# Second attention of a two-block model: head pairs in the value product, q packed as pairs, rope once for four heads

## Chip, cores and metric

One core of a Trainium2 chip runs the whole kernel. The metric is device time in microseconds (us); lower is better. The kernel before takes 1873.75 us (median of 3 runs).

## What is computed

The reference is two transformer-like blocks on 512 tokens of width 1024. The change lies in the causal attention of the second one: 16 heads, each with a query of 64 plain numbers and 32 that are turned by position (rope), a key of 64 plain numbers with 32 turned ones that all heads share, and a value of 64 numbers. Cut to this part:

```python
q = (rmsnorm_2(q_lat, q_norm_g[l]) @ w_uq[l]).reshape(B, S, 16, 64 + 32)
q_rope = rotary(q[..., 64:], positions)
q = jnp.concatenate([q[..., :64], q_rope], axis=-1)
kv = (rmsnorm_2(kv_lat, kv_norm_g[l]) @ w_ukv[l]).reshape(B, S, 16, 64 + 64)
k_nope, v = kv[..., :64], kv[..., 64:]
k_r = jnp.broadcast_to(rotary(k_rope, positions)[:, :, None, :], (B, S, 16, 32))
y_mla = causal_block_attention(q, jnp.concatenate([k_nope, k_r], -1), v)
merged = (jax.nn.sigmoid(g_rnn) * (y_rnn @ w_proj_rnn[l])
          + jax.nn.sigmoid(g_mla) * (y_mla @ w_proj_mla[l]))
```

## The kernel before

**Layout.** Activations lie transposed: 128 channels on the partitions, 512 tokens along the free axis, one such tile in one PSUM bank (`B[0]` to `B[7]`). `F(i)` and `R(i)` are the same SBUF tile `i` as fp32 and as fp32r.

**Blocks.** Every large product runs in blocks: one 128x128 weight block against 512 tokens, as three fp32r matmuls (high weights by high and by low activations, low weights by high activations: L251, L252, L253). The weights come as one stream in the order of use, 8 blocks a chunk, 286 chunks. For each chunk the SP queue loads `raw` (L2363), ScalarE (ACT) makes `whi` (L813), and VectorE (DVE, L1371) or, around the attention, GpSimd (POOL, L2150) makes `wlo`. `prep` and `start_of` set how far ahead each engine does this, and `until` does so for SP.

**Attention.** The order of work of each engine is written out by hand, head by head, `h` from 0 to 15. In head `h` TensorE (PE) turns the probabilities of head `h` (`mturn`, 4 groups of transposes, L653), multiplies them by the values (`mtimes`, key blocks 0 to 3, L667: two records for each fp32 matmul) and computes the scores of head `h+1` (`mscore`, L638, and the mask L640, token blocks `n` = 3, 2, 1, 0 with 512, 384, 256 and 128 keys). Between these stand 8 blocks of other products (`side`): the q projection of head `h+2` (`up_q`, 3 blocks), for every second head the k projection of two heads (`up_k`, 2 blocks), and the gate projection (`fill`), 64 blocks over the whole attention. DVE finds each score's maximum (`mmax`, L2014), ACT takes the exponential (`mexp`, L1236), DVE divides by the sum (`mnorm`, L2020 and L2021). Scores alternate between banks 3 and 4, so `mscore(h+1, 1)` waits until `mexp(h+1, 3)` has read bank 3.

**q and its rope.** `up_q(h)` makes one head: 96 rows used of 128, an odd head with rope rows 0 to 31 and plain rows 64 to 127. `q_copy` (ACT, L1214) brings all 128 rows to `QM[h % 2]`; then `mrope(h)` makes four DVE instructions on 32 rows (L2005, L2006, L2008, L2009) before bank 0 may be used again. `mnorm(h+1, 0)`, for which the next `mturn` waits, stands behind `mrope(h+2)` on DVE.

**Values.** `mtimes(h, kb)` writes partitions 0 to 63 of bank 7 for an even head and 64 to 127 for an odd one. After each odd head ACT and DVE take bank 7 away as the high and the low part of `YM` (`ym_hi` L1263, `ym_lo` through L1398). Transposed probabilities go through three buffers `PTM`, copied by ACT (L1249) and DVE (L2030).

**After it.** `first_pm` begins the output projection during head 15, and then `merged` is formed in `GMLA`: L2072 multiplies, L2075 adds the recurrent branch, which had been stored to `spare2` and is loaded into tiles `GR2` (L2454: six tiles after `until("uq", 8)`; L2459: two tiles after `until("pm", 2)`). The residual is loaded by L2463 right behind those.

Of the kernel before, what the change touches and what calls it, by code (L numbers as in the profile page):

```python
# [22 lines left out]
NCHUNK = 286  # L23
# [28 lines left out]
for _sem, _kinds in {  # L52
# [7 lines left out]
        "lru_dve": "lru_m lru_b lru_xv lru_h conv krsh kr_set",  # L60
# [87 lines left out]
QM, KM, PM, PTM, RM = (70, 71), (75, 78), 34, (39, 40, 41), (79, 74)  # L148
GR2 = [24, 25, 26, 27, 28, 29, 70, 71]
# [19 lines left out]
def program(nc, blocks, wst, xT, pT, small, consts, pos1, pos2, cT, wadaT, bcmp, ccmp, gblk, spare, spare2, us, ys, out):  # L169
    ctx = ExitStack()  # L170
    with ctx:
# [64 lines left out]
        def tensor(e):  # L236
# [358 lines left out]
            def up_q(h, ks):  # L595
                if ks[0] == 0:
                    if h == 0:
                        e.wait_ge(*at("pr_ev", 0))
                        for k in range(3):
                            e.wait_ge(*at("oplo", "ql", k))  # L600
                    else:
                        e.wait_ge(*at("mshq", h - 1))
                proj("uq", h, B[0], QL, ks)

            def up_k(h, ks):
                if ks[0] == 0:
                    if h == 0:
                        e.wait_ge(*at("pr_ev", 1))
                    else:
                        e.wait_ge(*at("km", h - 1))  # L610
                proj("uk", h // 2, B[1], KL, ks)

            def fill(n):
                for f in range(fills[0], fills[0] + n):
                    if f % 8 == 0 and f < 64:
                        if f:
                            e.wait_ge(*at("gmla", f // 8 - 1))
                        else:
                            e.wait_ge(*at("pr_ev", 2))
# [4 lines left out]
            def mscore(h, n):  # L624
                bk, w = B[3 + (n + 1) % 2], (n + 1) * 128
                K = slice(0, 96) if h % 2 == 0 else slice(0, 128)
                if n == 3:
                    e.wait_ge(*at("kr_set"))
                    e.wait_ge(*at("mrope", h))
                    e.wait_ge(*at("km", h))  # L630
# [24 lines left out]

            def mtimes(h, kb):
                rows_ = slice(64 * (h % 2), 64 * (h % 2) + 64)
                c0 = kb * 128
                e.wait_ge(*at("mptv" if kb == 1 else "mpt", 4 * h + kb))
                if kb == 0 and h % 2 == 0 and h:  # L660
                    e.wait_ge(*at("oplo", "ym", h // 2 - 1))
                if h == 0 and kb == 0:
# [3 lines left out]
                vo = h % 8 * 64  # L666
                e.matmul(B[7][rows_, c0:512], F(VS[h // 8][kb])[:, vo:vo + 64], F(PTM[(4 * h + kb) % 3])[:, c0:512],  # L667
                         start=kb == 0, stop=True, skip_group_check=True).then_inc(*sig("mpv", h, kb))

            def side(h, x):  # L670
                if h % 2 == 0:
                    if x < 2:
                        up_k(h, [x])
                    elif x < 5:
                        up_q(h, [x - 2])
                    else:
                        fill(1)
                elif x < 3:
                    up_q(h, [x])
                else:  # L680
                    fill(1)
# [3 lines left out]
            up_k(0, [0])  # L685
            up_k(0, [1])
# [9 lines left out]
            up_q(1, [0, 1, 2])  # L696
# [3 lines left out]
            def first_pm():  # L700
                f = pms[0]
                pms[0] += 1
                if f == 0:
                    e.wait_ge(*at("mshq", 15))
# [5 lines left out]
            for h in range(16):  # L710
                def work(x):
                    if h < 14:
                        side(h + 2, x)
                    elif h == 14:
                        fill(1)
                if h < 15:
                    work(0)
# [4 lines left out]
                    work(1)  # L722
                    mtimes(h, 0)
                    mscore(h + 1, 1)
                    work(2)
                    mscore(h + 1, 0)
                    work(3)
                    mturn(h, 2)
                    mtimes(h, 1)
                    work(4)  # L730
                    work(5)
                    mturn(h, 3)
                    work(6)
                    mtimes(h, 2)
                    mtimes(h, 3)
                    work(7)
# [68 lines left out]
        def scalar(e):  # L805
# [403 lines left out]

            def q_copy(h):  # L1210
                e.wait_ge(*made("uq", h))
                if h >= 2:
                    e.wait_ge(*at("msc", h - 2, 0))
                e.activation(F(QM[h % 2]), B[0], ACT.Copy).then_inc(*sig("mq", h))  # L1214

            def k_copy(h):
                e.wait_ge(*made("uk", h // 2))
                for x in (h, h + 1):
                    if x >= 2:
                        e.wait_ge(*at("msc", x - 2, 0))  # L1220
                    rows_ = slice(64 * (x % 2), 64 * (x % 2) + 64)
# [1377 lines left out]
```

## Time and profile before

| | us |
|---|---|
| median of 3 runs (1873.26 to 1876.18) | 1873.75 |
| profiled execution, own time | 1876.76 |
| its span, first to last instruction | 1875.0 |
| TensorE busy in the span | 1851.1 |
| VectorE busy | 1058.8 |
| ScalarE busy | 753.8 |
| GpSimd busy | 276.3 |

The granted TensorE clock is 0.997 of full speed over the span. Matmuls are pipelined: a record's duration covers its latency too, so the cost of a matmul is the distance from its start to the next start, and that distance is how the timeline of PE is read.

### The profile page before, as it was taken

How to read it: one execution, taken by the hardware profiler on the slowest of the kernel's cores; microseconds unless marked ns; L12 is line 12 of the kernel's file. 1: busy time of each engine (PE TensorE's matmuls, PEld its weight loads, DVE VectorE, ACT ScalarE, POOL GpSimd, SP SyncE). 2: the span in 40 equal slices, each digit the busy share in tenths (PEclk: the TensorE clock that was granted, in tenths of full speed). 3: DMA queues.
4: the chain of work that ended last, by engine and by line, in shares of the span. 5: the costliest groups of instructions: out<-in, count | busy, mean ns of one | idle time of the engine just before them, and what ended most of it. 6: DMA issues, size and time to landing. Idle time of an engine off the chain costs nothing.

```text
span 1875.0 us, 21232 instructions
## 1 busy us (share of the span) xinstructions
PE 1851.1 (99%) x8304; PEld 1454.5 (78%) x8304; DVE 1058.8 (56%) x1574; ACT 753.8 (40%) x1192; POOL 276.3 (15%) x357
## 2 busy tenths in 40 slices
PE   9999999999999999999999999999999999999998
PEld 7888888778878888888877767666668788888886
DVE  8764553846575545553577592555535565435643
ACT  6554444443352212222434653444433344324431
POOL 4767535200000000000001021321210000000000
PEclk9999999999999999999999999999999999999999
DMA  5323222224235535542423223212114223233321
GB/s 208 102 74 96 68 85 88 83 86 156 91 128 203 193 133 205 194 152 78 140 73 109 78 79 118 96 34 79 46 44 148 79 92 100 79 106 97 90 83 63
DMA packets 64403, 199.44 MB, mean 106 GB/s; under 512 B 7152, under 2 KB 11504, under 8 KB 64304
## 3 DMA queue, kind: packets, MB, share of 16 engines
q1 hardware_dynamic: 64304, 198.09, 32.1%
q8 instruction: 66, 1.08, 0.2%
q14 instruction: 33, 0.27, 0.0%
HBM read 189.68 MB, written 8.39 MB: 106 GB/s over the span
## 4 chain that ended last, share of the span: by engine, by line
PE 71%; issue 21%; DVE 6%; ACT 2%; DMA 0%; POOL 0%; SPq 0%; POOLq 0%; DVEq 0%; ACTq 0%
PE bank L251 20%; PE bank L253 20%; PE bank L252 20%; PE bank L638 2%; PE bank L667 2%; PE bank L653 1%; DVE wlo L1371 1%; PE bank L544 1%; PE bank L297 1%; PE bank L340 1%; PE bank L356 1%; DVE tiler L1398 1%; DVE tile L1906 1%; ACT whi L813 0%; PE bank L377 0%
## 5 line engine op out<-in xcount | busy, mean ns | idle before, releaser
L251 PE MATMUL bank<-tiler,whi 128*128 128x512 f32 x2272 | 917.8, 404 | 6.7 <-DVE wlo L1371 1.5
L253 PE MATMUL bank<-tiler,wlo 128*128 128x512 f32 x2272 | 897.1, 395 | 0.0
L252 PE MATMUL bank<-tiler,whi 128*128 128x512 f32 x2272 | 896.6, 395 | 0.0
L813 ACT ACTIVATE whi<-raw 128x1024 fp32r<-128x1024 f32 x285 | 300.1, 1055 | 605.6 <-PE bank L253 599.3
L251 PEld LDWEIGHTS bank<-tiler,whi 128*128 128x128 f32 x2272 | 427.2, 188 | 126.7 <-issue 21.2
L253 PEld LDWEIGHTS bank<-tiler,wlo 128*128 128x128 f32 x2272 | 427.0, 188 | 102.1
L252 PEld LDWEIGHTS bank<-tiler,whi 128*128 128x128 f32 x2272 | 427.7, 188 | 97.0 <-issue 3.1
L1371 DVE TENSOR_TENSOR wlo<-raw,whi 128x1024 fp32r<-128x1024 f32 x262 | 325.4, 1246 | 281.9 <-ACT whi L813 281.5
L2159 POOL TENSOR_TENSOR stat<-stat,scl 128x4 f32<-128x4 f32 x7 | 7.8, 1111 | 1127.6 <-DVE stat L1389 698.4
L2150 POOL TENSOR_TENSOR wlo<-raw,whi 128x1024 fp32r<-128x1024 f32 x23 | 54.5, 2371 | 249.2 <-ACT whi L813 249.2
L2098 DVE SCALAR_TENSOR_TENSOR tile<-bank,sm,tile 128x511 f32<-128x511 f32 x44 | 33.0, 749 | 98.0 <-ACT tile L1345 62.5
L1398 DVE TENSOR_TENSOR tiler<-tile,tiler 128x512 fp32r<-128x512 f32 x109 | 73.9, 686 | 4.5 <-ACT tiler L1100 2.1
L823 ACT ACTIVATE tile<-tile 128x512 f32<-128x512 f32 x45 | 28.3, 629 | 102.2 <-DVE tile L2130 39.9
L1789 DVE CUSTOM_DVE_ANT_0 wide<-wide 128x1024 f32<-128x1024 f32 x48 | 58.5, 1220 | 0.0
L1236 ACT ACTIVATE wide<-bank,stat 128x512 f32<-128x512 f32 (+1 forms) x64 | 33.5, 525 | 46.7 <-DVE stat L2014 46.7
L2014 DVE TENSOR_REDUCE stat<-bank 128x1 f32<-128x512 f32 (+1 forms) x64 | 30.8, 489 | 31.8 <-PE bank L640 30.0
L638 PE MATMUL bank<-tile 96*128 96x384 f32 (+7 forms) x128 | 45.7, 452 | 0.0
L2130 DVE SCALAR_TENSOR_TENSOR tile<-bank,mod,tile 128x512 f32<-128x512 f32 x16 | 11.9, 751 | 58.8 <-PE bank L253 58.8
L667 PE MATMUL bank<-tile 128*64 128x512 f32 (+3 forms) x128 | 44.9, 452 | 0.0
L1818 DVE TENSOR_TENSOR tile<-tile,bank 128x512 f32<-128x512 f32 x22 | 15.1, 686 | 43.7 <-PE bank L253 41.0
L1345 ACT ACTIVATE tile<-bank,sm 128x512 f32<-128x512 f32 x22 | 17.1, 779 | 53.8 <-PE bank L253 53.8
L1832 DVE TENSOR_TENSOR tile<-tile,bank 128x512 f32<-128x512 f32 x16 | 11.0, 687 | 47.6 <-PE bank L253 47.6
(364 smaller groups left out, 1635.5 us busy)
## 6 DMA issues: line engine op xcount, KB each, us to landing
raw<-wst SPq DMA_DIRECT2D x285, 512.0 KB, 3.6
wide<-wadaT SPq DMA_DIRECT2D x48, 512.0 KB, 3.5
tile<-xT SPq DMA_DIRECT2D x16, 256.0 KB, 6.1
spare<-tile SPq DMA_DIRECT2D x16, 256.0 KB, 2.0
tile<-spare SPq DMA_DIRECT2D x16, 256.0 KB, 5.0
out<-tile SPq DMA_DIRECT2D x8, 256.0 KB, 2.0
tile<-gblk SPq DMA_DIRECT2D x5, 256.0 KB, 4.6
us<-tile SPq DMA_DIRECT2D x4, 256.0 KB, 2.0
```

What stands on the lines that cost most here:

```text
L251: e.matmul(bank, whi[:, o:o + 128], hi, start=start, stop=False)
L252: e.matmul(bank, whi[:, o:o + 128], lo, start=False, stop=False)
L253: e.matmul(bank, wlo[:, o:o + 128], hi, start=False, stop=stop).then_inc(*sig("blk", n))
L638: e.matmul(bk[:, 0:w], F(QM[h % 2])[K, n * 128:(n + 1) * 128], F(KM[h % 2])[K, 0:w], start=True, stop=True, skip_group_check=True)
L667: e.matmul(B[7][rows_, c0:512], F(VS[h // 8][kb])[:, vo:vo + 64], F(PTM[(4 * h + kb) % 3])[:, c0:512], start=kb == 0, stop=True, skip_grou ...
L813: e.activation(whi[:, c % NHL * W:(c % NHL + 1) * W], raw[:, c % NRAW * W:(c % NRAW + 1) * W], ACT.Copy).then_inc(*sig("hi", c))
L1236: e.activation(prob(h, n), B[3 + (n + 1) % 2][:, 0:w], ACT.Exp, bias=stat[:, ST_MM + z + n:ST_MM + z + n + 1], accum_out=stat[:, ST_MD + z ...
L1371: e.tensor_tensor(wlo[:, h:h + W], raw[:, c % NRAW * W:(c % NRAW + 1) * W], whi[:, h:h + W].bitcast(F32), SUB).then_inc(*sig("lov", c))
L1398: e.tensor_tensor(R(lo), src, R(hi).bitcast(F32), SUB).then_inc(*sig("oplo", name, k))
L1789: e.tensor_tensor_reduce(w, w, F(CR, 2), 1.0, 0.0, MUL, ADD, F(PART)[:, m:m + 1]).then_inc(*sig("ada", m))
L2098: then(e.scalar_tensor_tensor(out=F(t)[:, 1:512], in0=bk[:, 0:511], scalar=col("fcw", 44 + mt), in1=F(t)[:, 1:512], op0=MUL, op1=ADD))
L2150: e.tensor_tensor(wlo[:, h:h + W], raw[:, c % NRAW * W:(c % NRAW + 1) * W], whi[:, h:h + W].bitcast(F32), SUB).then_inc(*sig("log", c))
```

## The change

Four edits that belong together:

1. The q weights are cut differently. `up_q(p)` makes the plain rows of a pair of heads (8 pairs, 24 blocks), and `up_r(g)` makes the rope rows of four heads (4 groups, 12 blocks). Before there were 16 heads with 48 blocks. The weight stream has 285 chunks.
2. `rope4(g)` multiplies, shuffles and multiplies all 128 rope rows of four heads with three DVE instructions; `mrope(h)` is then one addition of 32 rows into `QM`. `q_copy` copies 64 rows. `mnorm(h+1, 0)` now stands right behind `mnorm(h+1, 1)`.
3. `mtimes` runs in odd heads only and takes both heads of the pair, one behind the other, for each key block. `PTM` has eight buffers, four for each head of a pair.
4. The blocks of `side` are dealt out anew: 8 in the heads 0 to 2, 4 to 6, 8 to 10, 12 and 14 (in head 14: 8 of `fill`), 5 in the heads 3, 7, 11 and 13. `GR2` gets other tiles, and all its eight loads stand after `until("pm", 2)`.

Head 15 and all that follows keep their order. The diff, cut; on TensorE:

```diff
-QM, KM, PM, PTM, RM = (70, 71), (75, 78), 34, (39, 40, 41), (79, 74)
-GR2 = [24, 25, 26, 27, 28, 29, 70, 71]
+QM, KM, PM, PTM, RM = (70, 71), (75, 78), 34, ((24, 25, 26, 27), (28, 29, 39, 40)), (79, 74)
+GR2 = [66, 65, 64, 63, 62, 70, 71, 75]
...
+            def up_q(p, ks):
                 if ks[0] == 0:
-                    if h == 0:
+                    if p == 0:
                         e.wait_ge(*at("pr_ev", 0))
+                    elif p % 2:
+                        e.wait_ge(*at("mq", 2 * p - 1))
+                    else:
+                        e.wait_ge(*at("mshq", p // 2))
+                proj("uq", p, B[0], QL, ks)
+
+            def up_r(g, ks):
+                if ks[0] == 0:
+                    if g == 0:
+                        e.wait_ge(*at("pr_ev", 2))
                         for k in range(3):
                             e.wait_ge(*at("oplo", "ql", k))
                     else:
-                        e.wait_ge(*at("mshq", h - 1))
-                proj("uq", h, B[0], QL, ks)
-
-            def up_k(h, ks):
+                        e.wait_ge(*at("mq", 4 * g - 1))
+                proj("ur", g, B[0 if g else 2], QL, ks)
+
+            def up_k(p, ks):
                 if ks[0] == 0:
-                    if h == 0:
+                    if p == 0:
                         e.wait_ge(*at("pr_ev", 1))
                     else:
-                        e.wait_ge(*at("km", h - 1))
-                proj("uk", h // 2, B[1], KL, ks)
+                        e.wait_ge(*at("km", 2 * p - 1))
+                proj("uk", p, B[1], KL, ks)
...
-                e.matmul(B[7][rows_, c0:512], F(VS[h // 8][kb])[:, vo:vo + 64], F(PTM[(4 * h + kb) % 3])[:, c0:512],
-                         start=kb == 0, stop=True, skip_group_check=True).then_inc(*sig("mpv", h, kb))
+                for x in (h - 1, h):
+                    rows_ = slice(64 * (x % 2), 64 * (x % 2) + 64)
+                    vo = x % 8 * 64
+                    e.matmul(B[7][rows_, c0:512], F(VS[x // 8][kb])[:, vo:vo + 64], F(PTM[x % 2][kb])[:, c0:512],
+                             start=kb == 0, stop=True, skip_group_check=True).then_inc(*sig("mpv", x, kb))
...
             def side(h, x):
-                if h % 2 == 0:
-                    if x < 2:
-                        up_k(h, [x])
+                if h == 14:
+                    if x:
+                        fill(2 if x == 7 else 1)
+                elif h % 2 == 0:
+                    if x < 3:
+                        up_q(h // 2 + 1, [x])
                     elif x < 5:
-                        up_q(h, [x - 2])
+                        up_k(h // 2 + 1, [x - 3])
                     else:
                         fill(1)
-                elif x < 3:
-                    up_q(h, [x])
-                else:
+                elif h in (1, 5, 9):
+                    if x < 3:
+                        up_r((h + 3) // 4, [x])
+                    else:
+                        fill(1)
+                elif x not in (3, 5, 7):
                     fill(1)
```

In the head loop of PE the four calls of `mtimes(h, kb)` now stand under `if h % 2`. On ACT:

```diff
                     mexp(h + 1, 1)
-                    if h % 2 == 1 and h < 14:
+                    if h % 2 == 0 and h < 14:
                         q_copy(h + 2)
                     mexp(h + 1, 0)
                     if h % 2 == 0 and h < 14:
-                        k_copy(h + 2)
+                        q_copy(h + 3)
                 pt_copy(h, 2)
                 if h % 2 == 0 and h < 14:
-                    q_copy(h + 2)
+                    k_copy(h + 2)
+                    k_copy(h + 3)
```

On DVE:

```diff
+            def rope4(g):
+                bank = B[0 if g else 2]
+                e.wait_ge(*made("ur", g))
+                if g:
+                    e.wait_ge(*at("mrope", 4 * g - 1))
+                e.tensor_tensor(F(RM[0]), bank, F(RC2), MUL)
+                e.stream_shuffle(F(RM[1]), bank, SHUF).then_inc(*sig("mshq", g))
+                e.wait_ge(*at("mshq", g))
+                e.tensor_tensor(F(RM[1]), F(RM[1]), F(RS2), MUL).then_inc(*sig("mrot", g))
+
             def mrope(h):
-                rr = slice(64, 96) if h % 2 == 0 else slice(0, 32)
-                w1, w2 = F(RM[0])[rr, :], F(RM[1])[rr, :]
-                e.wait_ge(*at("mq", h))
-                if h:
-                    e.wait_ge(*at("mrope", h - 1))
-                e.tensor_tensor(w1, B[0][rr, :], F(RC2)[rr, :], MUL)
-                e.stream_shuffle(w2, B[0][rr, :], SHUF).then_inc(*sig("mshq", h))
-                e.wait_ge(*at("mshq", h))
-                then(e.tensor_tensor(w2, w2, F(RS2)[rr, :], MUL))
-                e.tensor_tensor(F(QM[h % 2])[rr, :], w1, w2, ADD).then_inc(*sig("mrope", h))
+                to = slice(64, 96) if h % 2 == 0 else slice(0, 32)
+                of = slice(32 * (h % 4), 32 * (h % 4) + 32)
+                e.wait_ge(*at("mrot", h // 4))
+                if h >= 2:
+                    e.wait_ge(*at("msc", h - 2, 0))
+                e.tensor_tensor(F(QM[h % 2])[to, :], F(RM[0])[of, :], F(RM[1])[of, :], ADD).then_inc(*sig("mrope", h))
...
+            e.wait_ge(*at("kr_set"))
+            rope4(0)
             mrope(0)
             pr_out(5)
             mmax(0, 3)
...
             mmax(0, 0)
             mnorm(0, 1)
             mrope(1)
+            mnorm(0, 0)
             pr_out(7)
             for h in range(16):
-                mnorm(h, 0)
...
                     mmax(h + 1, 0)
+                    if h < 14:
+                        mrope(h + 2)
                     mnorm(h + 1, 1)
-                if h < 14:
-                    mrope(h + 2)
+                    mnorm(h + 1, 0)
+                if h in (1, 5, 9):
+                    rope4((h + 3) // 4)
```

On SP:

```diff
-            until("uq", 8)
-            for m in range(6):
+            until("pm", 2)
+            e.wait_ge(*made("in2", 31))
+            for m in range(5):
                 e.wait_ge(*at("sp%d" % m, 0))
                 e.dma_start(F(GR2[m]), spare2[m]).then_inc(*sig("sp%d" % m, 1, by=16))
-            until("pm", 2)
             e.wait_ge(*at("msc", 15, 0))
-            for m in range(6, 8):
+            for m in range(5, 8):
```

## Rows read from the trace of the kernel before

**Rows 1.** Busy time by stretch, the attention: PE, PEld, DVE, ACT, POOL, clock, DMA.
```profile
1180.00:1412.00 232.00, 229.91 (x991) 145.41 (x990) 123.17 (x301) 106.34 (x249) 44.56 (x19) 1.00 0.20 64
```

**Rows 2.** Timeline of PE, end of heads 0 and 1: start, duration, instruction.
```profile
1211.00 0.40 PE L252 MATMUL bank<-tiler,whi 128*128 128x512 f32 x1
1211.23 0.40 PE L253 MATMUL bank<-tiler,wlo 128*128 128x512 f32 x1
1211.75 0.66 PE L653 MATMUL bank<-ident,wide 128*128 128x128 f32 x4
...
1223.97 0.40 PE L253 MATMUL bank<-tiler,wlo 128*128 128x512 f32 x1
1224.21 0.60 PE L653 MATMUL bank<-ident,wide 128*128 128x128 f32 x4
```

**Rows 3.** Timeline of PE, value products of head 0.
```profile
1201.96 0.40 PE L253 MATMUL bank<-tiler,wlo 128*128 128x512 f32 x1
1202.29 1.07 PE L667 MATMUL bank<-tile 128*64 128x512 f32 x2
1203.29 0.70 PE L638 MATMUL bank<-tile 128*128 128x256 f32 x2
...
1208.83 0.40 PE L253 MATMUL bank<-tiler,wlo 128*128 128x512 f32 x1
1209.16 0.86 PE L667 MATMUL bank<-tile 128*64 128x256 f32 x4
1209.95 0.50 PE L251 MATMUL bank<-tiler,whi 128*128 128x512 f32 x1
1210.29 0.39 PE L252 MATMUL bank<-tiler,whi 128*128 128x512 f32 x1
```

**Rows 4.** All weight loads of L667: duration ns min/median/max.
```profile
L667 PEld LDWEIGHTS bank<-tile x128: 132/136/137, 1202.3 to 1400.3; 128*64 128x64 f32 x128
```

**Rows 5.** Waits in the attention (1165 to 1412): us in total, times, longest.
```profile
PEld bank L653 <- DVE wide L2021: 4.9, 8, 1.0
```

**Rows 6.** Timeline of PE, first transposes of head 0.
```profile
1198.99 0.66 PE L653 MATMUL bank<-ident,wide 128*128 128x128 f32 x4 [0.54 <-DVE wide L2021]
```

**Rows 7.** Timeline of PE, DVE and ACT, first scores of heads 4 and 5.
```profile
1237.39 1.02 PE L638 MATMUL bank<-tile 96*128 96x512 f32 x2
1238.26 0.22 PE L640 MATMUL bank<-maskb,identb 128*128 128x128 bf16 x1
...
1239.24 0.69 ACT L1236 ACTIVATE wide<-bank,stat 128x512 f32<-128x512 f32 x1 [1.05 <-DVE stat L2014]
...
1240.20 1.07 PE L667 MATMUL bank<-tile 128*64 128x512 f32 x2
...
1249.81 1.02 PE L638 MATMUL bank<-tile 128*128 128x512 f32 x2
...
1250.93 0.69 DVE L1398 TENSOR_TENSOR tiler<-bank,tiler 128x512 fp32r<-128x512 f32 x1 [4.09 <-ACT tiler L1263]
...
1252.26 0.69 ACT L1236 ACTIVATE wide<-bank,stat 128x512 f32<-128x512 f32 x1 [0.87 <-DVE stat L2014]
```

**Rows 8.** Last instruction of `mrope`: duration ns min/median/max over 16.
```profile
L2009 DVE TENSOR_TENSOR tile<-tile x16: 678/682/2805, 1177.0 to 1371.5; 32x512 f32<-32x512 f32 x16
```

**Rows 9.** Timeline of DVE, q rope and last step of head 5's softmax.
```profile
1258.70 0.69 DVE L2005 TENSOR_TENSOR tile<-bank,tile 32x512 f32<-32x512 f32 x1 [2.53 <-ACT tile L1214]
...
1261.72 0.29 DVE L2021 TENSOR_SCALAR wide<-wide,stat 128x128 f32<-128x128 f32 x1
```

**Rows 10.** Timeline of SP, DVE and ACT after head 15; L2459's landing times.
```profile
1404.01 0.85 SPq L2459 DMA_DIRECT2D tile<-spare  x2
...
1407.65 0.69 DVE L2075 TENSOR_TENSOR tile<-tile 128x512 f32<-128x512 f32 x1
...
1426.20 1.06 ACT L813 ACTIVATE whi<-raw 128x1024 fp32r<-128x1024 f32 x1 [3.47 <-PE bank L253]
...
DMA to landing us min/median/max: 3.7/4.3/4.8
```

More of the change, by code:

```diff
@@ L22 @@
 NTILE = 80
-NCHUNK = 286
+NCHUNK = 285
 HALF_PI = math.pi / 2
@@ L710, in tensor @@
             for h in range(16):
-                def work(x):
-                    if h < 14:
-                        side(h + 2, x)
-                    elif h == 14:
-                        fill(1)
                 if h < 15:
-                    work(0)
+                    side(h, 0)
                     mturn(h, 0)
@@ L721, in tensor @@
                     mturn(h, 1)
-                    work(1)
-                    mtimes(h, 0)
+                    side(h, 1)
+                    if h % 2:
+                        mtimes(h, 0)
                     mscore(h + 1, 1)
-                    work(2)
+                    side(h, 2)
                     mscore(h + 1, 0)
-                    work(3)
+                    side(h, 3)
                     mturn(h, 2)
-                    mtimes(h, 1)
-                    work(4)
-                    work(5)
+                    if h % 2:
+                        mtimes(h, 1)
+                    side(h, 4)
+                    side(h, 5)
                     mturn(h, 3)
[L733 to L736, printed above, removed]
+                    side(h, 6)
+                    if h % 2:
+                        mtimes(h, 2)
+                        mtimes(h, 3)
+                    side(h, 7)
                 else:
@@ L1207, in scalar, with pair @@
                 e.activation(F(GRNN[m]), F(GRNN[m]), ACT.Sigmoid).then_inc(*sig("grnn_s", m))
+            def pair(x, to, bank, kind, scale):
+                if x >= 2:
+                    e.wait_ge(*at("msc", x - 2, 0))
+                rows_ = slice(64 * (x % 2), 64 * (x % 2) + 64)
+                e.activation(F(to[x % 2])[rows_, :], bank[rows_, :], ACT.Copy, scale=scale).then_inc(*sig(kind, x))
             def q_copy(h):
[L1211 to L1214, printed above, removed]
+                e.wait_ge(*made("uq", h // 2))
+                pair(h, QM, B[0], "mq", 1.0)
             def k_copy(h):
                 e.wait_ge(*made("uk", h // 2))
[L1218 to L1221, printed above, removed]
-                    e.activation(F(KM[x % 2])[rows_, :], B[1][rows_, :], ACT.Copy, scale=SC2).then_inc(*sig("km", x))
+                pair(h, KM, B[1], "km", SC2)
             def mexp(h, n):
@@ L1265, in scalar @@
             start_of("pr", 4)
-            start_of("uk", 0)
-            k_copy(0)
-            q_copy(0)
+            start_of("ur", 0)
+            for h in range(2):
+                k_copy(h)
+            for h in range(2):
+                q_copy(h)
             start_of("pr", 5)
@@ L1273, in scalar @@
             mexp(0, 1)
[L1274 removed]
+            start_of("pr", 7)
             mexp(0, 0)
[L1276 to L1277 removed]
             for h in range(16):
[L1279 to L1282 removed]
+                if h % 2 == 0 and h < 14:
+                    start_of("uq", h // 2 + 1)
+                elif h in (1, 5, 9):
+                    start_of("ur", (h + 3) // 4)
+                elif h < 15:
+                    start_of("in2", 24 + h // 2)
                 if h % 2 == 0 and h:
@@ L1289, in scalar @@
                     mexp(h + 1, 1)
-                    if h % 2 == 1 and h < 14:
+                    if h % 2 == 0 and h < 14:
                         q_copy(h + 2)
```

54 lines of the change are left out of this document (18 added, 36 removed).

## The prediction

> **What bounds the kernel.** I read part 1 of the page first: TensorE is busy for 1851.1 of 1875.0 us, and no other engine for more than 1058.8. The windows say the same of the stretch that is changed: from 1180 to 1412 us PE is busy for 229.91 of 232 us, DVE for 123.17, ACT for 106.34, at full clock [rows 1]. So the time is the sum of PE's own distances from start to start, plus the few places where PE waits. The timeline of PE gives the distances. Inside a block one matmul follows another after 0.23 us, and a transpose group that waits for nothing follows a block after 0.24 [rows 2]. A block of three is thus 0.70 us. Work taken from DVE or ACT buys nothing by itself; it counts only where one of them released PE late. The waits show one such place, the division by the sum (L2021) before the first transposes of a head, 8 times [rows 5].
>
> **Part 1, the blocks.** 48 q blocks become 24 + 12 = 36. Twelve blocks at 0.70 us are 8.4 us. All stood in PE's gapless stream, so nothing hides them: -8.4 us. They fall out of heads 3, 7, 11 and 13, three each, at places where the softmax of the next head has been issued; these heads get two heads' value products in exchange, so they do not become short. The ScalarE and DVE share of the one or two chunks fewer is off the path: 0.
>
> **Part 2, the value products.** Now every head pays for three visits to L667. The first: block to L667 0.33 us instead of 0.23, then 1.00 us to the next start [rows 3]. The third, 256 + 128 columns: again 0.33, then 0.79, and the block behind it has 0.34 instead of 0.23 between its first two starts [rows 3]. What the columns themselves take I scale from the 512-column score, 0.87 us from L638 to its mask [rows 7]: 0.87 for the first visit, 0.65 for 384 columns. So a visit costs beyond its columns 0.10 + 0.13 = 0.23 us for the first, and 0.10 + 0.14 + 0.11 = 0.35 for the third. The second also has 384 columns; behind transposes I take 0.27 (without the 0.08 that leaving any fp32 work costs). That is 0.85 us a head. Two heads in one visit pay it once: 8 x 0.85 = -6.8 us. Bounds: 0, if changing from one half of the array's columns to the other costs as much as entering, and -6.8.
>
> Then the columns. Each matmul is two passes with a weight load of 0.136 us each [rows 4]. Head A's second pass must follow its first, since both use the same columns of the array. Head B writes the other 64 partitions, so B's first pass could run beside A's second: three pass times instead of four. The trace of before never has two such neighbours, so it shows neither this nor its absence. Bounds from rows: nothing, or one pass of every key block, half of 0.87 + 0.65 + 0.65 = 1.08 us a pair, 8.7 us in all. Between them lies the case that B's weights are loaded only when A's second pass has started: each key block then saves its pass less 0.14, which is 0.29, 0.18 and 0.07 us for 512, 384 and 256 columns and nothing for 128, 0.54 us a pair, -4.3 us. I take this one, because a value product's records lie as load, matmul, load, matmul, and 0.136 us is longer than a 128-column pass.
>
> The Trainium skill bears on both halves. TensorEngine Tiling (Array Packing), section Key Properties, says that a change of tiling mode drains the array, while tiles of one mode work independently; by that page the first half is right and the second is the gain of up to 8.7 us. TensorE: Matmul & The Clock Gate, Part 3 (What overlaps and what doesn't), says against it that a weight load overlaps running matmuls only where the row groups differ, and here both heads use all 128 rows; by that rule alone the columns give nothing. The excess of 0.10 to 0.14 us around L667 agrees with the drain [rows 3].
>
> **Part 3, rope and the old waits.** `mrope` was four DVE instructions of about 0.68 us [rows 8] behind a copy, and the last division waited for it: PE's last start of head 0 is 1211.23, the transposes start 0.52 us later instead of 0.24, and take 0.05 longer to start up [rows 2]. About 0.33 us, in the 7 such heads that the waits count besides the first [rows 5]: 2.3 us. Before head 0 the idle time is 0.54 us at the least [rows 6], with the same start-up and pipeline loss about 0.8; there `mnorm(0, 0)` now goes before `pr_out(7)`. Together -3.1 us (bounds -2.4 and -3.5). `rope4` is three instructions of 128 rows at some 0.7 us (the rows are parallel, the length is the same 512), in heads 1, 5 and 9 only, with several us until the next `up_q` of an even pair needs its bank. Two such instructions were held for 2.8 us once each [rows 8]; the slack below covers one.
>
> **Part 4, a new wait.** In an even head nothing stands any more between `side(h, 1)` and `mscore(h+1, 1)`, which needs `mexp(h+1, 3)`. In head 3 the value product that stood there started 2.81 us after the head's first score [rows 7], so the score would now be due after 2.7. ACT begins the exponential 1.85 us after the score, takes 0.69 and about 0.1 for the sum: 2.64, and with a weight load of 0.2 behind it PE loses about 0.2 us. In head 4 it begins only after 2.45 us, because DVE first makes the low part of `YM` (1250.93) [rows 7]: 3.24, a loss of 0.75. This delay stays where the head before has 8 blocks and its gate copy stands at the end (heads 2, 6, 10); after the 5-block heads it is hidden. 3 x 0.75 + 5 x 0.2 = +3.3 us (bounds 0 and 8 x 0.75 = 6).
>
> Behind that score nothing else of PE is late: an even head lasts 12.4 us now (1237.39 to 1249.81 [rows 7]), less 3.0 for its value products 9.4, plus the wait. Head 5's softmax ends 12.2 us after its first score, but DVE was free at 1258.70 - 2.53 = 1256.17, 6.4 us after it [rows 7, 9]. With one rope addition, the last division and the late start that is about 8 us, and the next transposes come after 9.0 to 9.7.
>
> **Part 5, loads of `GR2`.** Eight loads now start at about 1404.0 instead of two. The first lands 4.3 to 4.8 us later, 1408.3 to 1408.8, where L2075 wanted it at 1407.65 [rows 10]. DVE is up to 1.2 us late with an addition; PE needs only L2072, already done, of the banks: 0. Six more issues at 0.43 us delay the residual and the next weights by 2.6 us and by what their bytes take; ScalarE wants the weights in question at 1426.20, 22 us after the first issue, some 3 us earlier now that chunks end half a chunk later. If the six landed one after the other at 4.8 us each, 29 us, the loss would be up to 10 us; but two landed in the time of one. I take 0.
>
> **Sum.** -8.4 - 6.8 - 4.3 - 3.1 + 3.3 = -19.3 us, from the profiled execution's 1876.76 to 1857.5. That execution lies 3.0 us above the median of 1873.75, so the forecast is 1854.4 us. A measurement of this kernel can tell about 0.2% (3.7 us) from no change.
>
> **Rivals.**
> (a) The pair shares its visit, but not its time: no overlap of the columns, 1858.7. For it: both heads fill all rows, and PE starts its matmuls in order. Chance 0.25.
> (b) A full pass saved in each key block: 1850.0. For it: a load lies ahead of its matmul elsewhere too. 0.17.
> (c) The change of column half costs what the entry cost; neither saving exists: -8.4 - 3.1 + 3.3 = -8.2, 1865.5. The rows show the excess at each side of L667 and never within one half. 0.12.
> (d) Slower. The softmax chain, not PE, sets the length of even heads, because `q_copy(h+2)` waits for `up_q`'s third block and holds back `mexp(h+1, 0)`. If the chain kept its 12.2 us against the 9.1 at which it is due, 8 even heads would lose 3.1 us each, 25 us, and the kernel would end at about 1879. It decides from (19.3 + 3.7)/8 = 2.9 us of lateness per even head; against it, the chain held two copies and four rope instructions and now holds one copy and one addition. 0.03, and 0.03 more for a part of it that lands within 0.2%.
> (e) The weights after the `GR2` loads come late by up to 10 us: about 1864. 0.05.
> My forecast has 0.35.
>
> **Range.** 1849 to 1863 us holds the forecast, (a), (b) and the bounds of parts 3 and 4 about them; outside lie (c), (d) and half of (e). Faster by over 0.2%: 0.94, within: 0.03, slower: 0.03.
>
> **What would show it.** In the profile after: 36 fewer records each of L251 to L253 together (12 each), 49 visits to L667 turned into 25, and in an even head `mscore(h+1, 1)` as the only place with a wait, 0.2 or 0.75 us. Part 2 is read from the start distances of a pair's first visit: with 512 columns twice, about 1.87 us for (a), 1.6 for the forecast, 1.45 for (b), over 1.95 for (c). The 0.52 us before the transposes must be 0.24, and the next weights must arrive without idle time of PE between 1400 and 1430. The prediction is wrong if an even head lasts over 11 us, or if that first visit lasts 2 us.

## The result and the profile after

| | before | after |
|---|---|---|
| median, us | 1874.78 (4 runs, 1873.26 to 1876.18) | 1841.28 (4 runs, 1836.53 to 1841.46) |
| profiled execution, own time, us | 1876.76 | 1841.46 |

The ratio is 0.9817, 95% interval 0.9803 to 0.9831: 33.5 us less, where 19.3 were forecast, and 7.7 us below the lower end of the range. The direction was right; the size was not. In one series below the kernel before once took 2012.11 us, at a lower clock, and the pair-only kernel once 9313.93 us; the medians given are those of the other executions.

The stretch with the attention, in the windows of the kernel after (columns as in [rows 1]; it now holds some of what follows the attention too):

```profile
1180.00:1412.00 232.00, 230.57 (x1106) 161.44 (x1105) 118.80 (x279) 117.45 (x264) 40.72 (x18) 1.00 0.25 83
```

PE is as full as before and the clock is the same. It gets through 1106 matmul records in the 232 us where it had 991: the stretch is shorter because PE's own work is. So the difference has to be looked for in start distances. First visit of a pair's value products in head 1, and third visit, timeline of PE after:

```profile
1211.92 0.40 PE L253 MATMUL bank<-tiler,wlo 128*128 128x512 f32 x1
1212.25 1.08 PE L681 MATMUL bank<-tile 128*64 128x512 f32 x4
1213.26 0.70 PE L650 MATMUL bank<-tile 96*128 96x256 f32 x2
...
1218.82 0.40 PE L253 MATMUL bank<-tiler,wlo 128*128 128x512 f32 x1
1219.14 0.87 PE L681 MATMUL bank<-tile 128*64 128x256 f32 x8
1219.94 0.50 PE L251 MATMUL bank<-tiler,whi 128*128 128x512 f32 x1
1220.28 0.39 PE L252 MATMUL bank<-tiler,whi 128*128 128x512 f32 x1
```

L681 is the old L667. The first visit has four records and lasts 1.01 us from start to start; one head's two records lasted 1.00 [rows 3]. The third has eight and lasts 0.80; one head's four lasted 0.79. The forecast had 1.6 us for the first visit, and its most hopeful rival 1.45. The second head costs 0.01 us. Why is seen when the window is cut so narrow that only records which start between 1212.24 and 1212.30 are listed (PE), and in PEld's answer for the same visit:

```profile
1212.25 0.65 PE L681 MATMUL bank<-tile 128*64 128x512 f32 x2
```
```profile
1212.25 0.20 PEld L681 LDWEIGHTS bank<-tile 128*64 128x64 f32 x4 [0.36 <-issue]
```

Two of the four matmuls start within 0.06 us of each other: both heads' first passes. (They cannot be the two passes of one head: in the kernel before, the second record of a 512-column product starts 0.48 us after the first.) All four weight loads are over by 1212.45, 0.20 us after the visit's start, while the first passes, 0.65 us together, still run.

The old wait before the transposes [rows 2, 6] is gone in both places, with 0.23 and 0.24 us from the last block's start:

```profile
1199.51 0.40 PE L253 MATMUL bank<-tiler,wlo 128*128 128x512 f32 x1
1199.75 0.60 PE L665 MATMUL bank<-ident,wide 128*128 128x128 f32 x4
...
1208.79 0.39 PE L253 MATMUL bank<-tiler,wlo 128*128 128x512 f32 x1
1209.02 0.49 PE L665 MATMUL bank<-ident,wide 128*128 128x128 f32 x3
```

The new wait stands where part 4 put it, at `mscore(h+1, 1)`; timeline of PE in heads 0 and 2, then its row in the waits from 1165 to 1412:

```profile
1202.65 0.40 PE L253 MATMUL bank<-tiler,wlo 128*128 128x512 f32 x1
1202.89 0.67 PE L650 MATMUL bank<-tile 128*128 128x256 f32 x2
...
1224.34 0.40 PE L253 MATMUL bank<-tiler,wlo 128*128 128x512 f32 x1
1225.16 0.70 PE L650 MATMUL bank<-tile 128*128 128x256 f32 x2 [0.42 <-ACT wide L1254]
```
```profile
PE bank L650 <- ACT wide L1254: 1.4, 4, 0.4
```

Head 0 waits for nothing (0.24 us). Head 2 has 0.82, a loss of 0.58, and with the slower start behind it the head lasts 9.90 us from first score to first score instead of 9.28 in head 0, 0.62; heads 6 and 10 are like it, and head 14 loses 0.33: 2.2 in all.

What the kernel lost, added up from PE's starts between the first transposes of head 0 and the last value product: 201.45 us before, 166.87 after, -34.6.

| part | forecast | read from the trace after |
|---|---|---|
| 12 blocks | -8.4 | -8.4 |
| value products, visits and columns | -11.1 | -24.8 (8 x (1.10 + 1.00 + 1.00)) |
| late transposes, 7 heads | -2.3 | -2.3 |
| a wait of L251 for a gate copy in head 14 | not named | -0.85 |
| new wait | +3.3 | +2.2 |
| sum | -18.5 | -34.15 |

The three numbers in the second row are what a visit costs over a stream without it: the first 0.10 + 1.00, the third 0.10 + 0.79 + 0.11, both by [rows 3]; the second, behind transposes, 0.31 to its start and 0.79 to the block, less the 0.13 that the two transposes alone take (1205.22 to 1205.35), and 0.03 behind it. An even head without a wait agrees: 12.42 us from first score to first score in [rows 7] (1237.39 to 1249.81), 9.28 after in head 0 (1200.18 to 1209.46). What is left of the -34.6, 0.4 us, is not assigned. Outside this stretch the stall before head 0 [rows 6] gave back 0.7; of the 35.4 us between the two profiled spans the rest is +1.5 ahead of the attention, where a stretch at half clock is longer (see below), and -1.6 behind it, which is not assigned.

### The profile page after: what moved, and what is told of

The parts are those of the page before. It is cut to its first block, busy times and chain, and to the rows that moved or that the text cites. A ratio compares the mean times of both kernels' runs of the same rounds, so it can differ in the third digit from the quotient of the medians.

```text
span 1839.6 us, 21094 instructions
## 1 busy us (share of the span) xinstructions
PE 1815.2 (99%) x8268; PEld 1443.0 (78%) x8268; DVE 1032.6 (56%) x1528; ACT 751.9 (41%) x1191; POOL 271.5 (15%) x355
## 4 chain that ended last, share of the span: by engine, by line
PE 70%; issue 21%; DVE 6%; ACT 2%; DMA 0%; POOL 0%; SPq 0%; POOLq 0%; DVEq 0%; ACTq 0%
PE bank L251 20%; PE bank L253 20%; PE bank L252 20%; PE bank L650 2%; DVE wlo L1390 1%; PE bank L681 1%; DVE tiler L1417 1%; PE bank L544 1%; PE bank L297 1%; PE bank L665 1%; PE bank L340 1%; PE bank L356 1%; DVE tile L1925 1%; ACT whi L831 1%; DVE tile L1425 0%
## 5 line engine op out<-in xcount | busy, mean ns | idle before, releaser
L251 PE MATMUL bank<-tiler,whi 128*128 128x512 f32 x2260 | 911.2, 403 | 6.8 <-DVE tiler L1470 1.7
L251 PEld LDWEIGHTS bank<-tiler,whi 128*128 128x128 f32 x2260 | 425.3, 188 | 119.8 <-issue 14.9
L2179 POOL TENSOR_TENSOR wlo<-raw,whi 128x1024 fp32r<-128x1024 f32 x21 | 49.9, 2374 | 217.6 <-ACT whi L831 217.6
L2159 DVE SCALAR_TENSOR_TENSOR tile<-bank,mod,tile 128x512 f32<-128x512 f32 x16 | 11.9, 751 | 59.8 <-PE bank L253 59.8
L1364 ACT ACTIVATE tile<-bank,sm 128x512 f32<-128x512 f32 x22 | 17.1, 779 | 53.3 <-PE bank L253 53.3
L1357 ACT ACTIVATE tile<-bank,sm 128x512 f32<-128x512 f32 x22 | 17.1, 779 | 44.0 <-PE bank L253 44.0
```

The costliest lines, as they stand in the source:

```text
L251: e.matmul(bank, whi[:, o:o + 128], hi, start=start, stop=False)
L2179: e.tensor_tensor(wlo[:, h:h + W], raw[:, c % NRAW * W:(c % NRAW + 1) * W], whi[:, h:h + W].bitcast(F32), SUB).then_inc(*sig("log", c))
```

## The experiments

Lines and ratios are of each kernel itself; a ratio is to the kernel before in the same series. Where a difference to the changed kernel is given, it is to the repeat of it that is nearest.

**The changed kernel again**, twice, unaltered.

> The changed kernel, unchanged, as the base of the three others. All theories: 1841 us, within 3 us, since one execution of it already came out at 1836.5 with a shorter stretch of half clock.

> The changed kernel again, unaltered, so that the two others of this call stand beside it on the same chip: 1836 to 1843 us, since its executions so far scatter over that by the half-clock stretch of 3.4 or 6.8 us around 950 us.

1839.84 us, ratio 0.9803 (0.9786 to 0.9821), and 1839.37 us, 0.9813 (0.98 to 0.9826). Three series give -33.5, -36.0 and -35.2 us by their medians. Inside the attention the three traces of the changed kernel agree within 0.02 us (166.87, 166.87 and 166.89). Single executions of it lie between 1836.53 and 1842.39 us, and the windows show one thing that does a part of this and has nothing to do with the change: a short stretch at half clock in an earlier stage. Windows of before, then of after:

```profile
945.00:950.00 5.00, 5.00 (x41) 4.73 (x39) 4.11 (x6) 2.79 (x4) 0.00 (x0) 1.00 0.36 105
950.00:960.00 10.00, 9.31 (x54) 8.10 (x54) 4.98 (x10) 1.70 (x3) 1.98 (x2) 0.83 0.17 52
```
```profile
945.00:950.00 5.00, 5.00 (x37) 4.55 (x35) 4.33 (x8) 2.20 (x4) 0.00 (x0) 1.00 0.33 105
950.00:960.00 10.00, 10.00 (x50) 9.04 (x51) 3.27 (x8) 0.77 (x2) 1.98 (x2) 0.66 0.17 52
```

The column after POOL is the granted clock: 0.83 and 0.66 as the mean of these 10 us, so a part of them at the level of 1.2 GHz, after a stretch in which PE had no idle time. Full clock is missing for 1.7 us in the one and for 3.4 us in the other. So single medians are not compared below 2 us here; distances inside the attention are.

**Both heads into the same half of the array's columns.** The pair stays; both write partitions 0 to 63 of bank 7, so the second head's values overwrite the first's and `YM` is not formed rightly.

```diff
-                    rows_ = slice(64 * (x % 2), 64 * (x % 2) + 64)
+                    rows_ = slice(0, 64)
```

> The changed kernel, but both heads of a pair write partitions 0 to 63 of bank 7, so the two matmuls of a key block use the same columns of the array; visits, order and waits stay. The sums of the odd heads land in the wrong place and partitions 64 to 127 keep old numbers. Theory (both heads' passes run at the same time because they lie in different column halves): the columns of the second head come back, (0.87 + 0.65 + 0.65) x 8 = 17.4 us, so about 1858.7. Rival (the gain came from fewer visits and from other waits, not from overlap): no change, 1841. Of my forecast's case (half of the passes overlapped) nothing more than 4.3 us would come back: 1845.6.

1856.21 us, 0.9891 (0.9876 to 0.9906): 16.4 us over the changed kernel. Timeline of PE, the first visit of head 1:

```profile
1210.18 0.39 PE L253 MATMUL bank<-tiler,wlo 128*128 128x512 f32 x1
1210.50 1.93 PE L681 MATMUL bank<-tile 128*64 128x512 f32 x4
1212.36 0.48 PE L650 MATMUL bank<-tile 96*128 96x256 f32 x1
```

1.86 us instead of 1.01, with the same four records, weights and columns. Rival (a) had put 1.87 on this case. The two heads run beside each other because they write different halves. An odd head, from first score to first score, grows from 12.41 to 14.57 us, over eight pairs 17.3; the whole attention, from the first transposes to the last value product, takes 183.53 us instead of 166.87, 16.7 more, though head 14 no longer waits. So the overlap is worth 16.4 to 17.3 us, and the rest of the 24.8, 7.5 to 8.4, is what the shared visits are worth (forecast 6.8).

**The pairing alone undone.** Each head has its own three visits again; buffers, projections and rope stay as changed.

```diff
-                for x in (h - 1, h):
+                for x in (h,):
...
-                    if h % 2:
-                        mtimes(h, 0)
+                    mtimes(h, 0)
```

> The changed kernel with only the pairing undone: every head multiplies its own probabilities by its own values, in the places of the kernel before; weights, rope, blocks and buffers stay as changed. Theory: eight heads' three visits come back, 8 x (1.10 + 0.98 + 1.00) = 24.6 us, and the new waits of even heads (3 x 0.58 us) go, since a value product covers them again: +22.9, so 1864.2. Rival, the forecast's size (visits 6.8 and overlap 4.3, less new waits): +9, 1850.

1863.08 us, 0.9931 (0.9915 to 0.9947): 23.2 us over the changed kernel. With the new waits gone in it too (they cost 2.2), that is 25.4 for the pairing by itself. Its attention takes 189.50 us, 22.6 more, which with the 2.2 is 24.8, as from the distances.

**The twelve blocks back.** Three more matmuls of a block's size, with arbitrary operands into bank 0, at each of the twelve empty places of `side`.

```diff
+            def extra(h):
+                e.wait_ge(*at("mq", h + 2))
+                for _ in range(3):
+                    e.matmul(B[0], R(QL[0][0])[:, 0:128], R(KL[0][0]), start=True, stop=True, skip_group_check=True)
...
+                else:
+                    extra(h)
```

> The changed kernel with 12 more blocks' worth of matmuls: in heads 3, 7, 11 and 13, at the three places left empty, three fp32r matmuls of 128x512 each with operands that lie ready, into bank 0, whose content nobody reads then. They compute nothing that is used. Theory (a block is worth its 0.70 us, gapless): 12 x 0.70 = 8.4 us, 1840 + 8.4 = 1848.4. Rival (heads 3, 7, 11 and 13 have slack because something else sets their length): less than half of it, 1844 at most.

1847.45 us, 0.9863 (0.9844 to 0.9883): 7.6 and 8.1 us over the two repeats. In its trace heads 3, 7 and 11 last 12.42 us from first score to first score instead of 10.30, so three blocks cost 2.12 us where the forecast has 2.10. Part 1 holds.

**Within the third visit, head by head.** Instead of A2, B2, A3, B3 (head, key block) the program issues A2, A3, B2, B3.

```diff
+                        for x in (h - 1, h):
+                            for kb in (2, 3):
+                                one(x, kb)
```

> The changed kernel, but at the visit of key blocks 2 and 3 the four matmuls go head by head (A2, A3, B2, B3) and not key block by key block (A2, B2, A3, B3), in the seven pairs before the last. Theory 1 (matmuls start in program order, only neighbours in the two column halves overlap): A2 runs alone for 0.43 us, A3 beside B2, B3 alone for up to 0.21: 0.3 to 0.43 us more in each of seven visits, 2 to 3 us in all, and the visit lasts 1.1 to 1.25 us instead of 0.80. Theory 2 (each half has its own queue): nothing, 0.80 us. The visit in the timeline decides, the time alone is too coarse.

1840.73 us, 0.9823 (0.9807 to 0.9839): no difference. Timeline of PE, the third visit, and the records that start between 1218.96 and 1218.98 (the products stand in L673 here):

```profile
1218.96 0.88 PE L673 MATMUL bank<-tile 128*64 128x256 f32 x8
1219.76 0.50 PE L251 MATMUL bank<-tiler,whi 128*128 128x512 f32 x1
...
1218.96 0.44 PE L673 MATMUL bank<-tile 128*64 128x256 f32 x2
```

0.80 us again, and two passes start within 0.02 us of each other although three more passes of head A stand between them in the program. They are one of each head: the two passes of one 256-column product start 0.27 us apart in the kernel before. PE takes the first matmul of head B ahead of what it still has to do for head A. The premise that it starts its matmuls in order does not hold across halves.

**The pairing alone, on the kernel before.** `mtimes`, the eight buffers and the moved `GR2` loads are as changed; the q projection, the rope and the division stay as before.

```diff
-QM, KM, PM, PTM, RM = (70, 71), (75, 78), 34, (39, 40, 41), (79, 74)
-GR2 = [24, 25, 26, 27, 28, 29, 70, 71]
+QM, KM, PM, PTM, RM = (70, 71), (75, 78), 34, ((24, 25, 26, 27), (28, 29, 39, 40)), (79, 74)
+GR2 = [66, 65, 64, 63, 62, 70, 71, 75]
...
-                    mtimes(h, 0)
+                    if h % 2:
+                        mtimes(h, 0)
```

> The kernel before with only the pairing (two heads in one visit, eight buffers, the loads that these need moved): 48 q blocks, one rope per head and the old order of the division stay. Theory: -24.6 us, plus a new wait of 0.58 us in the seven even heads from 2 on, +4.1: 1874.8 - 20.5 = 1854.3. Rival, the forecast's size: -11.1 + 4.1 = -7, 1867.8.

1890.24 us, 1.0079 (1.0061 to 1.0097): slower than before, and 36 us from what was expected. It is kin to rival (d): the softmax chain, not PE, sets the length of the even heads. But what comes late is not the exponential behind a copy, as (d) had it; it is the division behind the rope. The waits of the attention, the timeline of DVE in head 4 and that of POOL and PE beside it:

```profile
PE bank L653 <- DVE wide L2024: 19.9, 8, 2.8
```
```profile
1261.04 0.69 DVE L2008 TENSOR_TENSOR tile<-bank,tile 32x512 f32<-32x512 f32 x1 [2.06 <-ACT tile L1219]
...
1263.14 0.68 DVE L2012 TENSOR_TENSOR tile<-tile 32x512 f32<-32x512 f32 x1
1263.85 0.16 DVE L2023 RECIPROCAL stat<-stat 128x1 f32<-128x1 f32 x1
1264.05 2.05 DVE L2024 TENSOR_SCALAR wide<-wide,stat 128x128 f32<-128x128 f32 x1
```
```profile
1263.29 2.73 POOL L2151 TENSOR_TENSOR wlo<-raw,whi 128x1024 fp32r<-128x1024 f32 x1 [7.11 <-ACT whi L818]
```
```profile
1263.01 0.40 PE L253 MATMUL bank<-tiler,wlo 128*128 128x512 f32 x1
1266.16 1.12 PE L653 MATMUL bank<-ident,wide 128*128 128x128 f32 x4 [2.75 <-DVE wide L2024]
```

In the shortened even head the four rope instructions stand ahead of the last division, and PE stands 3.15 us where it should have 0.24; this recurs in 7 heads, 2.9 us each, 20 us. Two things add up: the rope is late (it ends at 1263.82 and PE was ready at 1263.25), and the division, 0.29 us otherwise [rows 9], takes 2.05 while a GpSimd chunk of 2.73 us runs. It ends with that chunk, 0.08 us behind it. After such stops the clock falls as well, windows of the attention:

```profile
1200.00:1250.00 50.00, 43.29 (x193) 27.36 (x192) 31.31 (x73) 21.71 (x56) 8.15 (x4) 0.93 0.19 59
1250.00:1300.00 50.00, 42.85 (x186) 27.22 (x185) 28.01 (x62) 22.33 (x54) 10.21 (x4) 0.90 0.15 43
1300.00:1350.00 50.00, 43.27 (x201) 27.81 (x200) 30.02 (x70) 22.27 (x55) 9.95 (x4) 0.96 0.10 32
1350.00:1400.00 50.00, 45.32 (x206) 28.55 (x207) 28.56 (x70) 21.64 (x55) 7.74 (x4) 0.93 0.15 43
```

**Pairing with the division first.** The kernel above, with the last division of a head's softmax ahead of the rope of the head after next.

```diff
+            mnorm(0, 0)
...
             for h in range(16):
-                mnorm(h, 0)
...
+                    mnorm(h + 1, 0)
```

> The pair-only kernel (which came out at 1891.5, slower than before) with one more edit of the change: the last division of a head goes before the next q's rope on DVE, and mnorm(0, 0) before mrope(1). Theory (PE stood 2.9 us in each of seven even heads because the division stood behind the four rope instructions and was then held by GpSimd's chunk operation, 2.05 us instead of 0.29, and the clock fell after it): only the rope is left in the way of the next score, about 0.3 us a head, and no half clock: 1855 to 1860. Rival (the q rope of one head itself comes too late for a head of 9.4 us): PE stands at the next score instead, and the time stays above 1880.

1858.08 us, 0.9914 (0.9893 to 0.9935): one moved instruction pair is worth 32 us here. The traces take this apart. From the first transposes to the last value product this kernel needs 184.80 us and the one above 216.46, 31.7 more. The seven even heads with a stop are longer by 19.8 us together, from first score to first score. The seven odd heads behind them, which have no stop, are longer by 11.9 (13.8 to 14.1 us instead of 12.5 in five of them): the time at the level of 1.2 GHz falls there. Here no window of the attention is below full clock.

Two new waits are left, each 7 or 6 times 0.4 us by the waits (the one for the gate copy in head 14 is there too):

```profile
PE bank L251 <- DVE tile L2009: 2.8, 7, 0.4
PE bank L638 <- ACT wide L1241: 2.6, 6, 0.4
```

The first is `up_q` waiting for the rope's shuffle (0.80 us of start distance instead of 0.23, 7 times); with rope once for four heads it does not exist.

**The division first, on the kernel before.** The same edit without the pairing.

> The kernel before with one edit of part 3: the last division of a head's softmax ahead of the rope of the head after next. By the forecast's own terms the late starts of the transposes go, 7 x 0.33 + 0.8 = 3.1 us, so some 1871 to 1872 us against the kernel before of this call at its 1873 to 1877, ratio 0.9983. Rival: the rope is now later, so the q projection of the next head, which waits for its bank, or the first score of the head after is late, and the time stays or rises by up to 8 x 0.3 us.

1871.47 us, 0.9985 (0.9976 to 0.9994): -3.1 us, the forecast's number for this step. The division's wait is gone and the one for the gate copy in head 14 remains, so that one goes by the new order of the blocks. Its attention takes 199.07 us instead of 201.45, 2.4 less, where the forecast had 2.3 for the seven heads. Waits of the attention in this kernel:

```profile
PE bank L251 <- ACT tile L1259: 0.7, 1, 0.7
```

**A block ahead of the new wait.** In even heads a second block stands before `mscore(h+1, 1)`.

```diff
+                    if h % 2 == 0:
+                        side(h, 2)
                     mscore(h + 1, 1)
-                    side(h, 2)
+                    side(h, 3 if h % 2 == 0 else 2)
                     mscore(h + 1, 0)
-                    side(h, 3)
+                    if h % 2:
+                        side(h, 3)
```

> The changed kernel; in even heads one block more stands ahead of mscore(h+1, 1) (side 2 before it, side 3 between it and mscore(h+1, 0)). Theory (PE waits 0.58 us there in heads 2, 6 and 10 for the exponential that frees bank 3): that wait goes, nothing else is late: -1.7 us, about 1838.5. Rival (the wait moves to the next score, which needs the second exponential): no change, 1840.

1835.69 us, 0.9796 (0.978 to 0.9812). Timeline of PE, head 2:

```profile
1223.15 0.40 PE L253 MATMUL bank<-tiler,wlo 128*128 128x512 f32 x1
1223.39 0.60 PE L650 MATMUL bank<-tile 128*128 128x256 f32 x2
1223.82 0.22 PE L652 MATMUL bank<-maskb,identb 128*128 128x128 bf16 x1
```

The gap is 0.24 us in every even head. The whole attention (first transposes to last value product) takes 163.8 us instead of 166.9: 2.2 for the waits, and 0.1 in each of the eight heads, where the mask now follows the score after 0.43 us, against 0.53 in head 2 and 0.50 in head 0 of the changed kernel. That the score's weight load, which also waited for the exponential, is the cause of this 0.1 is likely and not shown.

**Two visits instead of three.** The same in even heads; in odd heads key blocks 0 and 1 of the value product stand together, behind a second block, `mscore(h+1, 1)` and a third block.

```diff
                     side(h, 1)
+                    side(h, 2)
+                    mscore(h + 1, 1)
+                    side(h, 3)
                     if h % 2:
                         mtimes(h, 0)
-                    mscore(h + 1, 1)
-                    side(h, 2)
+                        mtimes(h, 1)
                     mscore(h + 1, 0)
-                    side(h, 3)
                     mturn(h, 2)
-                    if h % 2:
-                        mtimes(h, 1)
```

> The changed kernel with the second score group and the fourth moved back in every head: in odd heads the value products of key blocks 0 and 1 stand together, so a pair makes two visits to the 64-column products instead of three, and in even heads two blocks stand ahead of mscore(h+1, 1). Theory 1 (a visit costs some 0.23 to 0.35 us for entering and leaving, whatever stands in it): the waits of heads 2, 6 and 10 go (3 x 0.58 = 1.7 us) and 8 visits go (8 x 0.25 to 0.35 = 2.0 to 2.8 us), together 3.7 to 4.5 us below the changed kernel of the same call. Theory 2 (the excess belongs to each change of the shape of the moving operand, so joining saves nothing): only the 1.7 us. The joined visit, 512 and 384 columns, should last 1.65 to 1.75 us from start to start, against 1.01 + 0.80 for the two apart.

1831.92 us (1831.72 to 1832.04), 0.9774 (0.976 to 0.9787): the best kernel of the study, 7.4 us under the changed one in the same series. Timeline of PE:

```profile
1210.20 0.40 PE L253 MATMUL bank<-tiler,wlo 128*128 128x512 f32 x1
1210.52 1.73 PE L681 MATMUL bank<-tile 128*64 128x512 f32 x8
1212.18 0.49 PE L650 MATMUL bank<-tile 96*128 96x128 f32 x2
```

The joined visit lasts 1.66 us. The attention takes 161.0 us: 2.8 less than with the block ahead alone. Head 15 keeps its order, so 7 visits are saved and not the 8 of the expectation: 0.40 each, a little over the 0.35 that theory 1 allowed. (Head 1 lasts 12.04 us from first score to first score, 12.43 with the block ahead alone.) Theory 2, no gain, is excluded; with the 3.1 us of the block this is 5.9 of the 7.4. The two profiled executions differ by 6.0 us; the other 1.5 are within what executions scatter.

## Why the prediction was wrong, and where it was right

**The failed step** is the one on the columns in part 2: "Head A's second pass must follow its first, since both use the same columns of the array. Head B writes the other 64 partitions, so B's first pass could run beside A's second: three pass times instead of four." B's first pass runs beside A's first, and B's second beside A's second: two pass times instead of four. Forecast at 4.3 us, the overlap measures 16.4 to 17.3. The step took for granted that PE hands out its passes in order of the program and that a weight load (0.136 us [rows 4]) holds up the next pass. The first visit and the head-by-head kernel show that the order does not bind across halves, and the narrow window that the loads of both heads run under the first passes. The second of these could be read before the change. In the first visit of head 0 [rows 3] PEld has

```profile
1202.28 0.19 PEld L667 LDWEIGHTS bank<-tile 128*64 128x64 f32 x2 [0.37 <-issue]
```

so the load of the second pass is over 0.19 us after the visit's start, and the second pass starts only 0.48 us after the first: it does not wait for its load. The upper bound fell with it: "one pass of every key block", 8.7 us, was half of what was possible, so neither the range nor any rival reached the result. A bound that asked what happens if the second head is wholly free (the 6.8 of the visits and 8 x (0.87 + 0.65 + 0.65) = 17.4 for the columns, 24.2 us, all from numbers of part 2) would have held it: 1873.75 - 8.4 - 24.2 - 3.1 + 3.3 = 1841.4.

The two rules of the Trainium skill that stood against each other are decided by the trace. TensorEngine Tiling (Array Packing), section Key Properties, lets tiles of one mode work independently: this trace agrees, with 1.01 us for four records. TensorE: Matmul & The Clock Gate, Part 3, lets a weight load overlap running matmuls only if their row groups differ. Here all four loads have 128 rows and end 0.20 us after the start, beside passes of the same rows, and in the row of the kernel before the same happens within one half. So the rule does not hold here, for two halves of the columns or for one.

**Part 1** was right: -8.4 forecast, 7.6 to 8.1 by the medians with the blocks put back, 2.12 us for three by the trace. **Visits** were near: 6.8 forecast, 7.5 to 8.4 left when the overlap is taken away, and 0.40 us for one visit fewer. **Part 3** was right, by the kernel that has this edit alone (-3.1; that it agrees to the tenth is luck, its interval is -1.1 to -4.5, and its trace has 2.4 where 2.3 was forecast). But what the edit is worth depends on the rest: with the pairing it is 32 us. The forecast argued against rival (d) with a chain that "now holds one copy and one addition". The pair-only kernel keeps the four rope instructions ahead of the division, and its even heads are late; with the division moved alone the stops are gone. **Part 4** was right in place and in kind, 2.2 us instead of 3.3. The 0.75 was meant for heads 2, 6 and 10 and came as 0.58 to 0.62; the 0.2 in the five others was 0.33 in head 14 and at most 0.1 in four. **Part 5** was right in its price of 0, though an addition of DVE was 2.1 us late and not the 1.2 that it allowed. The loads of `GR2` (L2484, L2488) stand together, by the timelines of SP and DVE,

```profile
1370.22 2.27 SPq L2484 DMA_DIRECT2D tile<-spare  x5
1372.59 1.55 SPq L2488 DMA_DIRECT2D tile<-spare  x3
```
```profile
1374.24 0.69 DVE L2104 TENSOR_TENSOR tile<-tile 128x512 f32<-128x512 f32 x1 [2.12 <-DMA tile<-spare]
```

and PE did not wait for it. **Not seen** was a wait in the kernel before: L251 in head 14 for the gate copy L1259, 0.85 us.

**The sum again**, with measured sizes: -19.3, another -13.7 for the value products, -0.85, -1.1 for the smaller wait: -35.0. The series gave -33.5, -36.0 and -35.2.

## What to carry to other kernels

Two matmuls that fill different halves of the array's columns, with the same number of rows, are as cheap as one: look for 64-column products in pairs, and put all pairs that are ready into one visit (0.40 us for each visit saved). When a resource could run beside itself, take "wholly free" as the upper bound, not the most plausible partial overlap. Pair, then look at what PE's lost time had been hiding: here the same pairing was worth -13 us (1858.08 against 1871.47) or +14 (1890.24 against 1875.85, the kernel before in that series), depending on whether one division stood ahead of or behind a rope.

## What the runs showed of the hardware that was not expected

- First passes of two fp32 matmuls that write different halves start within 0.06 us, in program order or not; a pair of 512 columns takes 1.01 us, the same four records in one half 1.86.
- The weight load of a product's second pass runs under its first pass, in one half too: 0.19 us for both loads of L667, with the passes 0.48 us apart.
- A DVE instruction of 128x128 (L2024) took 2.05 us instead of 0.29 beside a GpSimd instruction and ended 0.08 us after it. The trace does not tell what they shared.
- Stops of PE of 3 us in every second head lowered the granted clock of the stretch to 0.90 to 0.96; where they are gone it is 0.997 over the whole span. Of the 36 us by which that kernel missed its expectation the longer even heads are 20, the slower clock behind the stops 12, and the waits of `up_q` for the rope's shuffle, 7 times 0.56 us, 4.
